# A transformer block's prelude with half of the late modulation columns summed on GpSimd, two w_out slots split there, and b2 as two rows

## What is computed

```python
def first_block(x, c, w_in, w_out, sinks, rel_bias, w_ada, b_ada, norm_gains, w1, b1, w2, b2):
    c_act = jax.nn.silu(c)
    mod = c_act @ w_ada[l] + b_ada[l]                       # 6144 columns
    sh1, sc1, g1, sh2, sc2, g2 = [m[:, None, :] for m in jnp.split(mod, 6, axis=-1)]
    h = rmsnorm(x, norm_gains[l, 0]) * (1.0 + sc1) + sh1
    y = token_mixer(h, w_in[l], w_out[l], sinks[l], bias_hb)   # 16 heads, 8 causal, 8 windowed with sinks
    x = x + g1 * rmsnorm(y, norm_gains[l, 1])
    h = rmsnorm(x, norm_gains[l, 2]) * (1.0 + sc2) + sh2
    y = jnp.square(jax.nn.relu(h @ w1[l] + b1[l])) @ w2[l] + b2[l]
    x = x + g2 * rmsnorm(y, norm_gains[l, 3])
```

## Time and profile before

| | us |
|---|---|
| three runs | 1463.8, 1463.83, 1466.46 |
| median | 1463.83 |
| span of the profiled execution | 1462.3 |
| busy in it: PE, DVE, ACT, GpSimd | 1077.6, 410.3, 338.4, 18.6 |

### The profile page before, as it was taken

The page is one execution under the profiler, slowest core; times in us unless marked ns, Lnnn a source line. Parts: engine busy times, 40 slices in busy tenths (PEclk is TensorE's granted clock), DMA queues, the critical chain, the costliest instruction groups (busy, mean ns, idle before and its releaser), DMA issues.

```text
span 1462.3 us, 15804 instructions
## 1 busy us (share of the span) xinstructions
PE 1077.6 (74%) x6838; PEld 606.3 (41%) x6838; DVE 410.3 (28%) x766; ACT 338.4 (23%) x594; POOL 18.6 (1%) x38
## 2 busy tenths in 40 slices
PE   6999999999999999756566565565565565555555
PEld 3865788888989986211121111121111121111111
DVE  2557674656879864000000000000000000000001
ACT  2445563644644963000000000000000000000001
POOL 1200000000000000000000000000000000000000
PEclk9999999999999999987797787887868878778888
DMA  9989456563674589999999999999999999999996
GB/s 363 340 332 343 138 195 193 189 193 118 207 234 141 197 328 407 431 433 432 432 431 433 431 429 432 431 433 431 431 431 430 432 431 430 430 433 433 431 432 282
DMA packets 80783, 516.06 MB, mean 353 GB/s; under 512 B 6575, under 2 KB 46874, under 8 KB 63946
## 3 DMA queue, kind: packets, MB, share of 16 engines
q1 hardware_dynamic: 79168, 512.01, 86.1%
q0 software_dynamic: 1056, 2.43, 0.6%
q10 hardware_dynamic: 490, 0.61, 0.1%
HBM read 513.83 MB, written 1.07 MB: 352 GB/s over the span
## 4 chain that ended last, share of the span: by engine, by line
DMA 53%; PE 38%; DVE 6%; ACT 1%; issue 1%; SPq 0%; DVEq 0%; ACTq 0%
DMA expert_ring<-in_w_up_e 20%; DMA expert_ring<-in_w_gate_e 18%; DMA expert_ring<-in_w_down_e 15%; PE PS L623 6%; PE PS L1188 6%; PE PS L625 6%; PE PS L624 6%; PE PS L670 5%; PE PS L672 3%; DVE wR L382 2%; PE PS L1227 2%; PE PS L728 1%; PE PS L617 1%; DMA ring<-in_w_ada 1%; PE PS L697 1%
## 5 line engine op out<-in xcount | busy, mean ns | idle before, releaser
L1188 PE MATMUL PS<-expert_ring,xeT 128*32 128x512 f32 x2048 | 317.2, 777 | 228.3 <-DMA expert_ring<-in_w_up_e 121.8
L1188 PEld LDWEIGHTS PS<-expert_ring,xeT 128*32 128x32 f32 x2048 | 75.4, 138 | 466.2 <-issue 214.1
L1876 DVE TENSOR_TENSOR expert_rows<-expert_rows,PS 128x512 f32<-128x512 f32 x16 | 11.0, 688 | 807.8 <-PE PS L1188 807.8
L1227 PE MATMUL PS<-expert_ring,expert_rows 128*32 128x512 f32 x992 | 151.3, 759 | 100.3 <-DMA expert_ring<-in_w_down_e 98.1
L382 DVE TENSOR_TENSOR wR<-ring,wR 128x1024 fp32r<-128x1024 f32 x144 | 169.5, 1219 | 65.7 <-ACT wR L375 65.5
L375 ACT ACTIVATE wR<-ring 128x1024 fp32r<-128x1024 f32 x144 | 144.2, 1053 | 120.2 <-PE PS L625 120.1
L1227 PEld LDWEIGHTS PS<-expert_ring,expert_rows 128*32 128x32 f32 x992 | 38.0, 134 | 202.3 <-issue 110.2
L670 PE MATMUL PS<-hR,wR 128*128 128x512 f32 x320 | 112.6, 397 | 0.8 <-DVE wR L382 0.8
L672 PE MATMUL PS<-hR,wR 128*128 128x256 f32 x320 | 89.4, 279 | 0.0
L2248 ACT ACTIVATE selx<-PS 128x256 f32<-128x256 f32 x16 | 6.1, 383 | 326.7 <-PE PS L617 326.7
L623 PE MATMUL PS<-hR,wR 128*128 128x256 f32 x280 | 80.2, 286 | 0.8 <-DVE wR L382 0.8
...
## 6 DMA issues: line engine op xcount, KB each, us to landing
...
ring<-in_w SPq DMA_DIRECT2D x32, 1024.0 KB, 5.4
ring<-in_w_in SPq DMA_DIRECT2D x31, 1024.0 KB, 5.3
ring<-in_w_ada SPq DMA_DIRECT2D x24, 1024.0 KB, 9.5
ring<-in_w_out SPq DMA_DIRECT2D x8, 1024.0 KB, 10.5
...
```

What stands on the lines that cost most here:

```text
L1188: mm = nc.tensor.matmul(PS[32 * j:32 * j + 32, kind // 2, :], xeT[:, e // GROUP % 2, k, own], w[:, j // 2, j % 2, :, :], start=(k == 0), s ...
L1227: mm = nc.tensor.matmul(PS[32 * at:32 * at + 32, 3, :], hidT[:, c % 4, 2 * q + c // 4, :], w[c][:, 512 * half:512 * (half + 1)], start=(q ...
```

## The change

Columns 2048 to 3071 (g1) and 5120 to 6143 (g2) of the modulation no longer go through PE. The remaining late columns, 3072 to 5119 (sh2 and sc2), are 8 slots (`N_ADA12` 16 to 8), one per pair, the first ahead of the attention. The gain columns come as 16 pieces of 128x1024 (`load_gain`, 0.5 MB each) into three buffers (part of `ahead`, and `ybuf`). GpSimd multiplies each by its entry of silu(c) and adds it to `gain_sum` in two instructions of 128x512 (`add_gains`); partition 0 of `gain_sum` starts from the row of b_ada. A product of a 128x128 of ones with `gain_sum` (`spread_gain`) then sums over the partitions and spreads the result in one step. Eight pieces (g1) are added during w_in, eight (g2) after the attention's splits.

GpSimd also splits w_out slots 0 and 1 (`G.tensor_copy` and `G.tensor_tensor`, 128x1024 each, four times), behind the first `add_gains`, the bias copy and the key move. PE starts w_out slot 0, tile 0 ahead of the last `weigh_pair`. The four banks of PSUM for w_out change places. The bias reads move from GpSimd's queue to SP's. DVE's first gain on y waits for `gain_added` 32, since `ybuf` is one of the buffers; so does PE's turning of T2. b2 is kept as a rounded row and the remainder on partitions 0 and 32 (`b2R`), so that `seed_b2` is one fast product of 64 partitions. The gains of g2 are formed inside the MLP.

```diff
-N_ADA0, N_WIN, N_ADA12, N_WOUT, ... = 8, 9, 16, 4, ...
+N_ADA0, N_WIN, N_ADA12, N_WOUT, ... = 8, 9, 8, 4, ...
...
+            def load_gain(which, k):
+                n = 8 * which + k
+                if n >= len(gain_in):
+                    sp.wait_ge(gain_added, 2 * (n - len(gain_in) + 1))
+                first = (2 * D, 5 * D)[which]
+                sp.dma_start(gain_in[n % len(gain_in)], ada_rows[k, :, first:first + D])\
+                    .then_inc(gain_loaded[n % len(gain_in)], 16)
             for g, (dst, src) in enumerate(loads):
+                if g == G_WIN + 6:
...
+                    for k in range(3):
+                        load_gain(0, k)
+                if g == G_WIN + 7:
+                    sp.wait_ge(bias_stored, 16)
+                    for h in range(HEADS):
...
+                        sp.dma_start(biasm[:, h, 0:S], src_h).then_inc(bias_in, 16)
+                if G_WIN + 7 <= g < G_WIN + 7 + 5:
+                    load_gain(0, g - G_WIN - 4)
+                if g == G_MLP:
+                    for k in range(3):
+                        load_gain(1, k)
+                if g == G_MLP + 4:
+                    for k in range(3, 8):
+                        load_gain(1, k)
...
+            ada(G_ADA12, 0, 6)
             pe.wait_ge(win_out[0], 8)
             score_pair(0)
-            for p in range(HEADS // 2 + 2):
+            for p in range(HEADS // 2 + 1):
                 if p >= 2:
                     weigh_pair(p - 2)
-                if p < HEADS // 2:
-                    ada(G_ADA12 + 2 * p, 2 * p % 8, 6 + p // 4)
                 if p + 1 < HEADS // 2:
                     score_pair(p + 1)
+                if p == HEADS // 2:
+                    pe.wait_ge(modrow_set, 3)
+                    turn_mod(1, 7)
                 if 1 <= p <= HEADS // 2:
                     turn_pair(p - 1)
-                if p < HEADS // 2:
-                    ada(G_ADA12 + 2 * p + 1, (2 * p + 1) % 8, 6 + p // 4)
+                if p < HEADS // 2 - 1:
+                    ada(G_ADA12 + p + 1, p + 1, 6)
...
+            wout(0, 0)
+            weigh_pair(HEADS // 2 - 1)
+            wout(0, 1).then_inc(slots_used, 1)
             pe.wait_ge(att_split, HEADS // 2)
+            wout(1, 0)
+            wout(1, 1).then_inc(slots_used, 1)
+            pe.wait_ge(gain_added, 16)
+            spread_gain(0, 0)
+            pe.wait_ge(modcol_set, 2)
+            spread_gain(0, 1)
             wout(2, 0)
...
             dve.wait_ge(half_squared, 2)
+            dve.wait_ge(gain_added, 32)
...
+            def add_gains(which):
+                for k in range(8):
+                    n = 8 * which + k
+                    pool.wait_ge(gain_loaded[n % len(gain_in)], 16 * (n // len(gain_in) + 1))
+                    rows = gain_in[n % len(gain_in)]
+                    then(G.tensor_scalar(rows, rows, cact[:, k:k + 1], None, ALU.mult))
+                    for half in range(2):
...
+                        G.tensor_tensor(gain_sum[:, which, c], rows[:, c], gain_sum[:, which, c], ALU.add).then_inc(gain_added, 1)
+            add_gains(0)
             pool.wait_ge(bias_in, 16 * HEADS)
             G.tensor_copy(biasm[:, :, S:384], biasm[:, :, P:S]).then_inc(bias_copied, 1)
...
+            for g in range(G_WOUT, G_WOUT + 2):
...
+                    G.tensor_copy(halves(g, 0)[:, piece], slot(g)[:, piece]).then_inc(slot_rounded, 1)
...
+                    G.tensor_tensor(halves(g, 1)[:, piece], slot(g)[:, piece], halves(g, 0)[:, piece], ALU.subtract)\
+                        .then_inc(slot_split, 1)
+            add_gains(1)
```

186 lines of the change are left out of this document (97 added, 89 removed).

## The result

The changed kernel takes 1490.43 us (median of 4 runs, 1488.7 to 1491.32) against 1465.14 us for the kernel before on the same chip (1463.8 to 1471.76): a ratio of 1.016, 95% interval 1.014 to 1.019. It was forecast at 1456.6 us, in a range from 1450.5 to 1473. The profiled execution has a span of 1486.9 us, 24.6 more than before.

A forecast was written before the change was run, and what follows sets the result against it. PE was taken to bound the attention pairs (4.45 us), DVE 0.7 us behind. T2 8.1 us earlier and +0.9 behind it gave -7.2: span 1455.1, 1456.6 us against the median, range 1450.5 to 1473.

The forecast's parts named there:

- The attention bound by DVE: Attention: with a modulation slot gone from each turn, DVE binds instead of PE; 3.9 us per pair against 4.45.
- The price of the multiplication: GpSimd's gain rows: multiplying 1024 elements costs as much as a copy, 0.95 us, making a row 3.15 us.
- The two-input price: GpSimd's splits and sums: 1.90 us taken for a two-input instruction of 1024 elements, bounds 0.95 to 2.87.
- The path of GpSimd: Splits from 103.2 to 115.4, gain rows to 140.6, then DVE's gain: normed tile turned before the MLP (T2) at 146.5.
- PE's path: PE's w_out work behind the attention: T2 at 145.7, or 147.2 with 1.5 us for the clock, 12.5 us earlier.
- best end: Whole kernel without any hold and with the clock up: -14.0 + 0.9, giving 1450.7 us.
- The bias copy at nothing: Ahead of the attention: bias ready at 87.4, first logits at 90.66, cost 0, up to 5 us; late start 0.07.
- One hold per pair: Attention: a GpSimd instruction holds DVE's multiplications once per pair, four pairs x 1.1 us = 4.4; forecast's chance 0.60 (none to one).
- the first rival: Attention: GpSimd holds DVE one instruction at a time, 18 to 28 us in place of 4.4; 1474 us; chance 0.24.
- A slow GpSimd: Two-input GpSimd instructions at a third of the copy's rate put T2 at 158.1; 1463.2 us, no change; chance 0.09.
- Behind T2: In front of and inside the MLP: four fast seeds of 0.23 us come on top, +0.9 us.
- The rounding of b2 and DVE's small instructions ahead of the attention: Before the attention: b2's rounding, some 3 us, runs while DVE waits for PE's last w_in slot; cost nothing.

The follow-up runs named there:

- e1_bias_first: Changed kernel with GpSimd's attention bias copy moved behind the third gain row instead of the eighth; ratio 1.009 to the kernel before.
- e9_pool_adds: Kernel before plus twelve idle-buffer GpSimd sums of 128x1024 through the attention; one run, span 1476.7 us.
- e12_act_scales: Changed kernel without g2's rows, bias copied early, w_out splits on ACT and DVE, b2 rounded behind the attention, g1 multiplied on ACT; ratio 0.996 to the kernel before.
- e4_both: Changed kernel with the bias copy behind the third gain row and g2's rows in their own buffers; ratio 1.008 to the kernel before.

## Why the prediction was wrong, point by point

**The attention bound by DVE: right.** Without GpSimd beside it the pair takes 3.45 us, less than the 3.9 of the forecast.

**The price of the multiplication: wrong, the largest term.** "A gain row is one 1024 instruction and two of 512: 1.05 + 2 x 1.05 = 3.15" was the step that failed. It took a `tensor_scalar` to cost what the copy of the earlier trace rows costs. It takes 2.9 us, and a row 5.54 us on average (44.3 us for g2's eight). The two-input price was bounded and lay inside its bounds (2.35 against 0.95 to 2.87 for 1024 elements, with 1.90 taken; the forecast's 0.95 for 512 was 1.24); for the multiplication I had taken one value with no bound, because it has one tensor for an input like the copy. The Trainium skill, "GPSIMD Engine Reference", section 3.1, gives 4497 ns for a two-input add of 2048 elements; half of it, 2.25 us, is an estimate for 1024, and the 2.35 here agrees within 5%. That figure was nearer than my own value. It says nothing of a multiplication by a column.

**The path of GpSimd.** The formula held: 176.8 plus 5.9 is 182.7, and 182.8 was seen. What stands in front of it is late by: splits begun at 114.3 in place of 103.2 (11.1), 14.0 us of splits in place of 12.2 (1.8), a wait of 4.2 us for the first row of g2, and rows of 44.3 in place of 25.2 (19.1). That is 36.2 on 146.5, or 182.7. So T2 hung on GpSimd's own path and not on the holds beside PE's path, for which the forecast had added 4.4; DVE's wait of 12.19 us shows it. The holds act through this path, since they put off what releases GpSimd's loads. The forecast's best end, -14.0, had overlooked this path even with its own prices: it took PE's 145.7 where GpSimd's was 146.5.

**The bias copy at nothing: wrong.** "with 3.15 for the row and 1.90 for the copy the bias is ready at 87.4": it was ready at 101.2. The sum followed the loads and took GpSimd to keep up with them. The mechanism was named and given 5 us as its upper end; it cost 10.6. Eight rows of 5.4 to 7.8 us stand in front of it, some 7 of their 52.0 us because GpSimd is drawn out beside DVE, and the fourth waited for SP's 17.5 us of bias reads. By e1_bias_first 6.8 us of T2 are its share.

**One hold per pair: wrong.** The rule is the first rival's: beside GpSimd's sums, copies and casts, whatever DVE starts with two inputs in SBUF, or as one of these multiplications, as a rule waits until GpSimd's instruction ends. Its size in the attention was 7.7 us in six holds over three pairs, in place of 18 to 28, since the rows of g2 began only at the last pair. The rival's time, 1474, was too low for another reason, the rows' price. In e9_pool_adds the rule stands alone and costs 14 us.

Beside GpSimd's multiplication the rule does not hold as it stands. DVE's timeline of after, while GpSimd multiplies from 81.89 to 84.74:

```profile
83.12 0.23 DVE L1387 TENSOR_TENSOR lambc<-lambc 128x64 f32<-128x64 f32 x1
...
83.84 0.92 DVE L1392 TENSOR_SCALAR sinkneg<-sinkbc 128x8 f32<-128x8 f32 x1
```

A two-input instruction begins and ends inside it at its full speed (0.22 before), a later one is held to its end. By the first rival's rule the first, too, would have waited; here the measurement decides. Why one passes and another not, no run here shows.

**A slow GpSimd:** this rival was right that GpSimd's path would bind, but priced the wrong instruction. It put the two inputs at 2.87 us, more than the 2.35 measured, left the multiplication at 0.95, and so gave 1463.2.

**Behind T2: right.** +0.9 was forecast; T2 to T3 takes 186.0 in e12_act_scales against 185.2 before, +0.8, though that kernel has no rows of g2. In after it is +1.8.

**The rounding of b2 and DVE's small instructions ahead of the attention:** cost at nothing because DVE idled there before: right. They were held as well (1.25 us in place of 0.16), but with them in place the first logits came at 90.65 in e4_both, and moving b2 away brought nothing.

**The range** ended at 1473. The first rival would have needed the multiplication's true price: with rows of 5.54 in the forecast's own sum T2 comes at 165.6 without any hold or late start, some 6 us later than before.
